# Attention of a hybrid layer: another order of the pair steps, taps of the convolution moved to TensorE, and one multiplication of the top-k mask on ScalarE

## The reference, cut to what matters

```python
# attention: an indexer scores the keys, the best 256 causal keys of each query are kept
idx_score = where(causal, idx_score, -inf)
_, sel = lax.top_k(idx_score, 256)
s = einsum(q_lat, c_kv[sel]);  p = softmax(where(valid, s, -inf));  o = (p @ c_kv[sel]) @ w_uv
# convolution module, 256 channels, width 31
h = a * sigmoid(gate)
h = causal_depthwise_conv(h, conv_w) + conv_b
y_c = silu(layer_norm_over_channels(h, conv_ln_g, conv_ln_b))
# all three parts, then
mix = concat([y_a, y_b, y_c]) @ w_o
```

## Time and profile before

| | us |
|---|---|
| median of 3 runs | 1118.21 |
| lowest, highest | 1118.06, 1127.09 |
| profiled execution, its own time | 1117.91 |
| its span | 1116.1 |
| busy in the span: PE, DVE, ACT, POOL | 944.8, 690.5, 564.8, 398.5 |
| mean granted TensorE clock (1 is full speed) | 0.927 |

### The profile page before, as it was taken

The page is one execution under the profiler, slowest core; times in us unless marked ns, Lnnn a source line. Parts: engine busy times, 40 slices in busy tenths (PEclk is TensorE's granted clock), DMA queues, the critical chain, the costliest instruction groups (busy, mean ns, idle before and its releaser), DMA issues.

```text
span 1116.1 us, 15675 instructions
## 1 busy us (share of the span) xinstructions
PE 944.8 (85%) x4724; PEld 729.0 (65%) x4725; DVE 690.5 (62%) x990; ACT 564.8 (51%) x796; POOL 398.5 (36%) x241
## 2 busy tenths in 40 slices
PE   6999999687876778699992599999999999999920
PEld 5877888133443444488882478888887888888820
DVE  4259888985656664463757366688888854334316
ACT  4266576963644446650121265678777744324323
POOL 0000299999999980000000111222323221211116
PEclk8999999888978989999995599999999999999975
DMA  8441120000000000162433747999999988554254
GB/s 230 116 114 38 27 87 1 0 1 0 1 1 1 1 1 1 39 189 85 189 141 121 294 168 233 339 386 397 395 394 399 392 293 264 175 132 106 44 150 189
DMA packets 60972, 171.14 MB, mean 153 GB/s; under 512 B 17120, under 2 KB 31456, under 8 KB 48608
## 3 DMA queue, kind: packets, MB, share of 16 engines
q1 hardware_dynamic: 53584, 143.85, 34.7%
q0 software_dynamic: 7056, 25.69, 9.5%
q10 hardware_dynamic: 288, 1.05, 0.3%
HBM read 141.73 MB, written 26.21 MB: 150 GB/s over the span
## 4 chain that ended last, share of the span: by engine, by line
PE 44%; DMA 12%; DVE 7%; issue 4%; ACT 4%; POOLq 0%; POOL 0%; ACTq 0%; DVEq 0%; SPq 0%
PE ps L415 11%; PE ps L417 10%; PE ps L416 10%; DMA raw<-in_w_gate 10%; PE ps L687 3%; PE ps L696 2%; PE ps L711 2%; ACT probs L986 2%; DVE wlo L1521 2%; PE ps L814 1%; PE ps L763 1%; ACT whi L1070 1%; DVE sm L1389 1%; DMA xg<-x_d,idx_now 1%; PE ps L757 1%
## 5 line engine op out<-in xcount | busy, mean ns | idle before, releaser
L1521 DVE TENSOR_TENSOR wlo<-raw,whi 128x2048 fp32r<-128x2048 f32 x96 | 216.0, 2287 | 52.3 <-ACT whi L1070 51.4
L1070 ACT CAST whi<-raw 128x2048 fp32r<-128x2048 f32 x96 | 180.5, 1911 | 72.6 <-DMA raw<-in_w_gate 41.9
L415 PE MATMUL ps<-whi,xgT_hi 128*128 128x512 f32 x384 | 153.0, 398 | 6.9 <-DVE xgT_lo L1531 6.9
L417 PE MATMUL ps<-whi,xgT_lo 128*128 128x512 f32 x384 | 150.8, 393 | 0.0
L416 PE MATMUL ps<-wlo,xgT_hi 128*128 128x512 f32 x384 | 150.5, 392 | 0.0
L1329 DVE CUSTOM_DVE_ANT_0 probs<-ps,bias 128x128 f32<-128x128 f32 (+7 forms) x64 | 46.0, 755 | 83.1 <-PE ps L687 67.4
L415 PE MATMUL ps<-xT_hi,w_hi 128*128 128x512 f32 (+1 forms) x224 | 87.8, 392 | 4.8 <-DVE w_lo L1159 3.1
L1613 POOL TENSOR_SCALAR tapped<-hpad,par 128x1024 f32<-128x1024 f32 x30 | 89.5, 2984 | 2.9
L415 PEld LDWEIGHTS ps<-whi,xgT_hi 128*128 128x128 f32 x384 | 73.0, 190 | 23.0 <-issue 5.8
L1677 POOL COPY idx_now<-slot_token 128x1 int32 (+1 forms) x24 | 7.5, 313 | 223.2 <-PE ps L814 223.2
L416 PE MATMUL ps<-xT_lo,w_hi 128*128 128x512 f32 (+1 forms) x224 | 86.8, 388 | 0.0
(11 more groups left out here) (273 smaller groups left out, 1934.2 us busy)
## 6 DMA issues: line engine op xcount, KB each, us to landing
raw<-in_w_gate SPq DMA_DIRECT2D x32, 1024.0 KB, 12.5
raw<-in_w_up SPq DMA_DIRECT2D x32, 1024.0 KB, 12.4
raw<-in_w_down SPq DMA_DIRECT2D x32, 1024.0 KB, 10.7
w_raw<-in_w_in SPq DMA_DIRECT2D x14, 512.0 KB, 4.0
x_tok<-in_x SPq DMA_DIRECT2D x8, 512.0 KB, 7.5
wo_raw<-in_w_o SPq DMA_DIRECT2D x16, 256.0 KB, 2.7
x_res<-in_x SPq DMA_DIRECT2D x16, 256.0 KB, 3.4
x_d<-xa SPq DMA_DIRECT2D x4, 512.0 KB, 6.5
```

The lines of the kernel that those rows point to most:

```text
L415: pe.matmul(out, l_hi, r_hi, start=start, stop=False)
L417: return pe.matmul(out, l_lo, r_hi, start=False, stop=stop)
L1070: act.copy(whi[:, n, :], raw[:, n, :]).then_inc(gu_hi if n < 4 else dn_hi, 1)
L1521: dve.tensor_tensor(wlo[:, n, :], raw[:, n, :], f32(whi[:, n, :]), ALU.subtract).then_inc(gu_lo if n < 4 else dn_lo, 1)
```

## The change

The pair steps get another order: the scores of pair p+1 (p+2 among the short ones) stand ahead of the transposes of pair p, the products left over from pair p-1 come next, and ACT's two exponentials of pair p+1 stand one by one behind the second and third group of pair p. The ring has two banks in place of three, the finished products alternate between two banks, and the fourth group of block 7 is copied by DVE. Both heads' `qk` matmuls alternate by column chunk. Two choices go with each pair from the third on, and k6 is done by ACT. PE takes 24 taps of the convolution: up to 12 between the `key` and `val` units, the others up to 18 behind them, 6 behind the scores of the first two pairs. The reciprocal of the norm is taken of one column for each block (128x8 values) and spread by PE (`cb`). The units `key` and `val` use banks 0, 1, 2, 7.

```diff
-MIX_ORDER = [4, 5, 6, 7, 0, 1, 2, 3]
+MIX_ORDER = [4, 5, 0, 1, 2, 3, 6, 7]
-TAPS_PE = 18
+TAPS_PE = 24
+TAPS_EARLY = 18
+def groups(b):
+    return [range(k, min(k + 2, b + 1)) for k in range(0, b + 1, 2)]
     def scores(p):
-        for h in range(2):
-            steps.append(("qk", b, 2 * j + h))
-        rowsums(p - 1)
-        for _ in range(min(4 if p < 2 else 1 if p < SHORT_PAIRS else 2, len(choices))):
+        steps.append(("qk", b, j))
+        for _ in range(min(4 if p < 2 else 2, len(choices))):
             steps.append(choices.pop(0))
     scores(0)
     scores(1)
+    steps.extend(exponentials(0))
+    steps.append(("conv0",))
...
+    for p, (b, j) in enumerate(PAIRS):
+        while ahead < len(PAIRS) and ahead <= (p + 2 if p + 2 < SHORT_PAIRS else p + 1):
+            scores(ahead)
+            ahead += 1
+        if p and p - 1 == last_pair(PAIRS[p - 1][0]):
+            steps.append(("rl_set", PAIRS[p - 1][0]))
+        while waiting:
+            product()
+        exps = exponentials(p + 1)
+        for n in range(len(groups(b))):
+            by_dve = b == NT - 1 and n == 3
+            unit("pt", b, j, n, act=not by_dve, dve=by_dve)
+            if n == 0 and ended:
+                unit("rl", ended.pop(0), act=False, dve=True)
+            if n and exps:
+                steps.append(exps.pop(0))
             if len(waiting) == 2:
+                product()
             waiting.append((b, j, n))
+        steps.extend(exps)
+        if p == len(PAIRS) - 2:
             for c in range(2):
                 unit("cm", c, act=False, dve=True)
                 steps.append(("csq", c))
+    unit("cv", act=True, dve=False)
+    steps.append(("rl_set", NT - 1))
+    steps.append(("cr",))
     while waiting:
         product()
+    for c in range(2):
+        unit("cb", c, act=False, dve=True)
+    unit("rl", ended.pop(0), act=False, dve=True)
...
+        def unit_bank(k):
+            return ps[:, 4 + k % 4 if k < PROJECTIONS else (0, 1, 2, 7)[k % 4], :]
...  (TensorE)
+            for k, between in PLAN[1:]:
+                if k >= PROJECTIONS + 4:
+                    tap(taps)
+                    taps += 1
+                unit(k, between)
+            for w in range(taps, TAPS_EARLY):
+                tap(w)
...
-                        pe.wait_ge(masked_max, u - 3 if u < 2 * SHORT_PAIRS else u - 1)
+                        pe.wait_ge(masked_max, u - 2 if u < 2 * SHORT_PAIRS else u)
                     for c in range(0, WIDTH[b], 512):
+                        for h in range(2):
+                            last = pe.matmul(scores_at(u + h, WIDTH[b])[:, c:c + n], qT[rows, j, ...], keyT[rows, j, ...])
...
                 for t in range(NT):
+                    if i == 0 and t == 4:
+                        pe.wait_ge(mixed, 4 * NT)
+                        pe.wait_ge(ring_act, sum(RING_ACT))
+                        pe.wait_ge(ring_dve, sum(RING_DVE))
...  (ScalarE)
+                if kind == "choose" and step[2] == CHOICES - 1:
+                    act.wait_ge(picked, CHOSEN[b] + 1)
+                    act.activation(bias[:, AT[b]:AT[b] + w], tied[:, 0:w], ACT.Copy, scale=BIG).then_inc(chosen, 1)
...
+                    if k == 0:
+                        act.wait_ge(mixed, 4 * NT)
+                        act.wait_ge(ring_dve, sum(RING_DVE))
+                    if k == 6:
+                        act.wait_ge(conv_n, 3)
+                        (Silu of both channel halves into mix[:, 6], mix[:, 7])
...  (VectorE)
                 elif k == 5:
-                    link(dve.scalar_tensor_tensor(T, T, -1.0, A, ALU.add, ALU.add))
-                elif k == 6:
-                    link(dve.tensor_scalar(x, T, BIG, None, ALU.mult))
+                    dve.scalar_tensor_tensor(T, T, -1.0, A, ALU.add, ALU.add).then_inc(picked, 1)
...
+                        if b >= FIRST_TOPK and h == 0:
+                            dve.wait_ge(chosen, CHOSEN[b] + 1)
+                elif kind == "pt":
+                    dve.tensor_copy(pT[:, no % 3, 0:w], src[:, 0:w]).then_inc(ring_dve, 1)
+                elif kind == "cb":
+                    for i in range(2):
+                        ch = conv[:, i, c * 512:(c + 1) * 512]
+                        dve.tensor_tensor(ch, ch, src, ALU.mult)
```

More of the change, by code:

```diff
@@ L87, in score_no, with last_pair @@
     return 2 * PAIR_NO[b, h // 2] + h % 2
-def last_no(*blocks):
-    return max(PAIR_NO[b, j] for b in blocks for j in range(HEADS // 2))
+def groups(b):
+    return [range(k, min(k + 2, b + 1)) for k in range(0, b + 1, 2)]
+def last_pair(b):
+    return max(p for p, x in enumerate(PAIRS) if x[0] == b)
 def attention_steps():
-    pairs = PAIRS
     steps, ring, r_of = [], [], {}
@@ L108, in unit, with product, exponentials @@
         ring.append((act, dve))
[L110 to L114, removed]
     def scores(p):
-        b, j = pairs[p]
+        b, j = PAIRS[p]
         while choices and any(x[1] == b for x in choices):
             steps.append(choices.pop(0))
-        for h in range(2):
-            steps.append(("qk", b, 2 * j + h))
-        rowsums(p - 1)
-        for _ in range(min(4 if p < 2 else 1 if p < SHORT_PAIRS else 2, len(choices))):
+        steps.append(("qk", b, j))
+        for _ in range(min(4 if p < 2 else 2, len(choices))):
             steps.append(choices.pop(0))
-    def after_block(b):
-        unit("rl", b, act=False, dve=True)
+    def product():
+        b, j, n = waiting.pop(0)
+        steps.append(("pv", b, j, n))
+        if PAIR_NO[b, j] == last_pair(b) and n == len(groups(b)) - 1:
+            ended.append(b)
+    def exponentials(p):
+        return [("exp", PAIRS[p][0], 2 * PAIRS[p][1] + h) for h in range(2)] if p < len(PAIRS) else []
     scores(0)
     scores(1)
+    steps.extend(exponentials(0))
+    steps.append(("conv0",))
     for i in range(2):
@@ L647, in _, with tap @@
             pe.wait_ge(dve_set, 1)
-            for k, between in PLAN[1:]:
-                unit(k, between)
-            pe.wait_ge(unit_act, sum(BY_ACT))
-            pe.wait_ge(unit_dve, sum(BY_DVE))
-            pe.wait_ge(idx_relu, len(IDX))
-            pe.wait_ge(pads_set, 1)
-            for w in range(TAPS_PE):
+            def tap(w):
+                if w == 0:
+                    pe.wait_ge(unit_act, seen(BY_ACT, PROJECTIONS - 1))
+                    pe.wait_ge(unit_dve, sum(BY_DVE))
+                    pe.wait_ge(pads_set, 1)
                 pe.wait_ge(diag_set, w // TAPS_PER_ROUND + 1)
@@ L966, in _ @@
                 item(*p)
-            act.wait_ge(conv0_mm, 1)
-            act.activation(conv[:, 0, :], pair(2), ACT.Identity, bias=convb[:, 0:1]).then_inc(conv0, 1)
             for step in STEPS:
@@ L1009, in _ @@
                 elif kind == "cv":
[L1010 to L1019 removed]
+                    act.activation(crstd[:], src[:, 0:NT], ACT.Sqrt, bias=eps).then_inc(ring_act, 1)
+            act.wait_ge(ring_mm, len(RING_ACT))
             act.wait_ge(ring_act, sum(RING_ACT))
[L1021 removed]
             for n in range(2 * KT):
```

232 lines of the change are left out of this document (112 added, 120 removed).

## The result

The changed kernel takes 1108.66 us (median of 4 runs, 1107.44 to 1109.54) against 1118.24 for the kernel before beside it: ratio 0.9894, 95% interval 0.9845 to 0.9944. The gain is 10 us. The forecast was 1079, a gain of 39, and the time lies outside its range. The profiled execution took 1109.54, with a span of 1107.8.

The account below looks back on a forecast made before the run. Latency was taken to rule around attention, each engine waiting for another. Stretches summed to a first projection at 434.7 against 474.2, -39.5 us; 1117.9 - 39.5 = 1078.4, stated as 1079. 8 in 10 between 1065 and 1103.

Parts of the forecast that it names:

- Start of attention: From the search's end to pair 2's mask: DVE starts at 250.3 instead of 260.7, pair 2's mask 3.1 us earlier.
- Long pairs, periods: Blocks 4 to 7: scores-to-scores periods of 4.6, 5.2, 6.2 and 6.8 us, set by PE alone.
- Rival B: Long pairs: ACT still paces them, old periods stay and only the choices' stalls go, 1103; chance 0.14.
- Short pairs: Pair 2's mask to block 4's: DVE paces with 50 us of work plus 4 of waits, 54; bounds 45 and 66.
- the sentence that the multiplication holds all behind it on ScalarE: Start of attention: everything behind the multiplication in ACT's queue waits for DVE; block 3's k5 ends at 259.5.
- DVE waiting for `chosen`: A sign that would show the forecast wrong: DVE waits for `chosen`; no size given.
- `rl` at 1.6 each: Long pairs: four `rl`, each with a wait for DVE's product, 1.6 us each, 6.4 in all.
- the tail from the last product: From the products' end at 428.6 to the first projection at 434.7: about 6.1 us.
- The sum: Whole kernel: first projection at 434.7 against 474.2, so -39.5 us, giving 1078.4, stated as 1079.
- Rival C: Short pairs: each of 16 steps k2 to k5 waits for a whole POOL scaling, +40 us, 1119; chance 0.06.
- Rival D: Long pairs: TensorE's clock at the lower level makes 91 us 182, 1170; milder form 1095; chance 0.05.
- The forecast's own sign: Block 4: the forecast is wrong if the clock there stays at 0.8.

Follow-up runs that it names:

- version 2: Changed kernel with `rl_set` moved ahead of the next scores, masks and choices at the end of a block; 1099.08 us, ratio 0.9841.
- version 3: version 2 with ScalarE's k6 placed behind the exponentials of its iteration; 1090.22 us, ratio 0.9752.
- version 5: version 3 with an iteration's two choices placed behind its `rl` unit instead of ahead of it; 1080.57 us, ratio 0.966.
- version 5 to 7: From version 5 to version 7: one choice with each short pair instead of two; 1080.57 us, then 1070.33 us.
- experiment 8: Changed kernel with GpSimd's convolution taps cut to 16 of 1024 columns; 1069.29 us, comparable only up to the first projection, which came 21.8 us earlier.
- version 7: version 3 with choices behind `rl` and one choice with each short pair instead of two; 1070.33 us, ratio 0.9567.
- second and third edit: Second: k6 behind its iteration's exponentials, on version 2, 1090.22 us. Third: choices behind `rl`, on version 3, 1080.57 us.
- versions of the table that take 646.0 to 647.7 us: Changed kernel with k6 back on VectorE, 1104.49 us; version 2 with k6 on VectorE, 1094.23 us; version 3, 1090.22 us.
- 6: version 3 with one choice with each short pair instead of two, choices still ahead of `rl`; 1083.39 us, ratio 0.9685.

## Why the prediction was wrong, by its steps

- **Start of attention: right**, to within the 4 us by which it varies. First mask 248.9 (250.3), pair 2 at 268.2 (268.6). The six late taps took 11.75 (10.3 to 12), and DVE waited 8.3 us.
- **Long pairs, periods: right.** 4.37, 5.02, 5.98, 6.63 against 4.6, 5.2, 6.2, 6.8. Rival B (ScalarE paces them, 1103) fell with this.
- **Short pairs: DVE's work right, the waits wrong.** "50 plus 4 us of waits" became 49.9 plus 15.3: the stretch took 65.2 instead of 54, 11.2 of the missing time. The forecast had the sentence that the multiplication holds all behind it on ScalarE, and used it for the first mask only, not for k6 of the blocks that follow. It looked for DVE waiting for `chosen`; what waited was ScalarE, for `tied`, 19.9 us.
- **`rl` at 1.6 each: wrong.** The step priced TensorE's wait for DVE's product alone. `rl_set` stands behind the scores' choices, and TensorE waited 20.7 us for it in six waits; behind five of them the clock fell. Block 4 to block 5 took 28.8 where 4 x 4.6 + 1.6 = 20.0 were forecast. There `rl_set` was only the first of three stops at one place: with it moved the stretch took 29.1, with k6 late 24.6, and with the product of `rl` ahead of the choices 19.1. The next stretches took 25.2 and 25.6 against 22.4 and 26.4, and the last, from block 7's first mask to the projection, 50.2 against the 43.3 that the forecast leaves: there two masks of 1.2 us stand ahead of `rlrep`, and behind that wait of 1.74 us the clock was at 0.50; `cm` took 3.70 and not 2.0, and the tail from the last product 7.6 and not 6.1, at a clock of 0.50 up to `rl`.
- **Behind the projection: not forecast.** From the first projection to the end before took 641.9 us and after 644.6, by the clock (below).
- **The sum.** -0.4 to pair 2, +11.2 short pairs, +17.7 long pairs and tail, +2.8 behind: 31.3, and 1109.5 - 1078.4 is 31.1.

By stretches (us, profiled runs):

| stretch | forecast | changed | version 2 | version 3 | version 5 |
|---|---|---|---|---|---|
| short pairs, to block 4's mask | 54 | 65.2 | 62.8 | 58.7 | 57.3 |
| to block 5's | 20.0 | 28.8 | 29.1 | 24.6 | 19.1 |
| to block 6's | 22.4 | 25.2 | 20.2 | 20.2 | 20.2 |
| to block 7's | 26.4 | 25.6 | 24.2 | 24.2 | 24.2 |
| to the projection | 43.3 | 50.2 | 46.6 | 46.2 | 48.3 |

Shown by experiment, in the stretch from first mask to first projection and each on top of those before it: `rl_set` behind the choices cost 11.4 us, ScalarE's queue behind k6 9.6, the ring bank held by `rl` 4.2, together 25.2 of the 28.9 that the short and long pairs and the tail were late. In another order the shares would differ, as block 4 shows. With all three mended the kernel takes 1080.6, and its projection comes at 438.8 (434.7); that the time is still only 1.6 above the forecast is in part luck, as behind the projection it takes 2.0 us less than the kernel before. The long pairs and the tail then take 111.7 (112.1), with single stretches up to 5 us off either way; the short pairs stay 3.3 above their 54. The forecast priced the list as if it had these places. A fourth point it took for harmless: two choices in each short pair cost 11.0 us of that stretch against one (version 5 to 7).

Rival C (each choice waits for a whole scaling, 1119) came near in the time but fell in its mechanism: the five steps k0 and k2 to k5 took 49.8 us, against 49.0 before. GPSIMD Engine Reference, Key points, in the Trainium skill says that GpSimd contends with VectorE where it has two SBUF inputs or a two-port mode; by that the two-input steps shrink without GpSimd and k0 does not, and experiment 8 agrees (1.66 to 0.95, 0.94 to 0.94). Rival D (the clock) was there as a follower: 0.77 and 0.82 in the short pairs and in block 4, and 1.00 in both in version 7, where the long waits are gone (0.88 and 0.99 in version 5). The forecast's own sign, a clock in block 4 that stays at 0.8, had come true.

Open: what the second and third edit would give alone on the changed kernel (only the first was tried alone), what the early start is worth to a microsecond, as 3.3 us is within the spread of the runs, and what the 3.3 us are that the short pairs take beyond the forecast in version 5.

## What to carry to other kernels

Work that is spread into an engine's queue is free only for what stands ahead of it: go through each step that one list issues, and write down for every small instruction that another engine waits for (a reciprocal, a product that frees a bank) what long work stands directly ahead of it. A share moved to another engine puts that engine's whole queue behind the first one's progress, so its place is behind what others wait for. And fewer buffers in a ring make each late release a stop: ask of every ring user, not only of the frequent ones, who frees its buffer and from where in which queue. Last, several stops can lie at one place: to take away the one that the profile names may give nothing until the next is gone too, as block 4's 28.8, 29.1, 24.6 and 19.1 us show.

## What the runs showed of the hardware

**A long wait can cost twice, by the clock.** The changed kernel right behind TensorE's wait of 6.61 us, by windows (columns as in the stages), and then, in the chain, the scores of that pair and of a later one of the same block:

```profile
344.80:348.30 3.50, 3.50 (x18) 2.51 (x18) 0.69 (x1) 1.56 (x5) 3.40 (x2) 0.50 0.03 5
```

```profile
348.39 2.44 PE ps L701 x8
...
356.34 1.28 PE ps L701 x8
```

The work behind the wait ran at 0.50, the 1.2 GHz level, and the scores took 2.44 us where they take 1.28 at 1.00. Of TensorE's six waits for `rlrep` in this trace, the five of 1.71 to 6.61 us had the clock down to between 0.50 and 0.66 within the 5 us behind them; behind the sixth, 1.25 us, it stayed at 1.00. Over the short pairs the granted clock was 0.77, and 1.00 in version 7, where the same 284 instructions took TensorE 9.3 us less.

**The clock can also differ far behind the change.** The routing's matmuls, the same in both kernels, before and after (window of some 105 us behind the projection):

```profile
L763 PE MATMUL ps<-sm,x1T 128*128 128x16 f32 x112 | 12.9, 258 | 0.0
```

```profile
L785 PE MATMUL ps<-sm,x1T 128*128 128x16 f32 x112 | 16.1, 290 | 0.0
```

3.2 us, with the granted clock at 0.80 instead of 1.00 in the 10 us in which it falls. Over all 128 of them (the windows above cut off 16) they ran at a mean of 286 to 287 ns in the versions of the table that take 646.0 to 647.7 us behind the projection and in the changed kernel, and at 258 in versions 2, 5, 6 and 7, with 639.9 to 640.8. So they hold about half of the 6 us. What decides between the two is not known. The timed runs of versions 3 and 5 lie close together (1080.41 to 1080.84 for version 5), so their medians seem to hold it too: of the 9.7 us that version 5 gained on version 3, some 5.5 would be this. That is argued from one profiled run of each version, and the two ran on different chips. Version 2 has both: its four runs took 1094.6, 1095.6, 1102.6 and 1103.4 us, and its median of 1099.1 lies between the two groups; the profiled one is the fastest. So for this kernel two medians some 5 us apart need a look at where in the trace the difference lies.

**GpSimd is slowed as well.** Its 1024-wide scaling takes 2.84 us at 346.92 in the changed kernel, and 4.62 beside DVE's scan of 3.69. **Alternating the heads gives nothing:** the scores of a pair of block 7 take 1.92 us, as before.
